# One encoder layer on one core: a gate row multiplied inside the expert loop, the closing norm shared out over three engines, and work moved into three gaps of TensorE

## The reference

```python
u = modulate(rmsnorm(x, norm_mix_g), sh_mix, sc_mix)
q, k, v, xr, yr, fr = split(u @ w_in)
y_na  = neighbourhood_attention(q, k, v, na_rpb)       # 512 channels
y_lru = rglru(conv(xr)) * gelu(yr)                     # 512 channels
y_f   = fourier_mix(fr)                                # 512 channels
g_na, g_lru, g_f = split(sigmoid(u @ w_branch_gate + b))
merged = g_na*(y_na @ w_proj_na) + g_lru*(y_lru @ w_proj_lru) + g_f*(y_f @ w_proj_fnet)
x = x + gt_mix * (merged @ w_out)
u2 = modulate(rmsnorm(x, norm_ffn_g), sh_ffn, sc_ffn)
x = x + gt_ffn * moe_ffn(u2)      # 32 experts, two for each token: w0*y0 + w1*y1
return rmsnorm(x, final_g)
```

## Time and profile before

| | |
|---|---|
| runs shown | 1743.59, 1745.26, 1745.7 us, median 1745.26 |
| profiled execution | 1744.06 us, span from first to last instruction 1742.4 us |
| TensorE busy | 1561.1 us (90%), mean granted clock 0.952 |
| VectorE, ScalarE, POOL busy | 670.7, 480.5 and 518.0 us |
| chain that ended last | PE 82%, DVE 8%, DMA 5%, issue 2% |

### The profile page before, as it was taken

The page is one execution under the profiler, slowest core; times in us unless marked ns, Lnnn a source line. Parts: engine busy times, 40 slices in busy tenths (PEclk is TensorE's granted clock), DMA queues, the critical chain, the costliest instruction groups (busy, mean ns, idle before and its releaser), DMA issues.

```text
span 1742.4 us, 36278 instructions
## 1 busy us (share of the span) xinstructions
PE 1561.1 (90%) x14696; PEld 1125.5 (65%) x14696; DVE 670.7 (38%) x1113; ACT 480.5 (28%) x816; POOL 518.0 (30%) x471
## 2 busy tenths in 40 slices
PE   3899999999979998999999982999999989999950
PEld 3677786777768786878877871555565555555530
DVE  4555534555553244453227743112112111111228
ACT  4465534444631110111013100222222222222214
POOL 3522232423433332233212201233232323323232
PEclk9899999999989999999999975999999999999985
DMA  9560012222123333431206129499999999989745
GB/s 310 157 225 24 25 53 72 70 73 72 38 85 108 114 89 114 150 106 36 89 18 192 49 102 392 163 400 400 400 401 400 399 400 400 400 312 401 280 143 212
DMA packets 177395, 343.10 MB, mean 197 GB/s; under 512 B 30528, under 2 KB 98496, under 8 KB 177296
## 3 DMA queue, kind: packets, MB, share of 16 engines
q1 hardware_dynamic: 144864, 281.90, 44.0%
q0 software_dynamic: 23712, 42.93, 7.4%
q10 hardware_dynamic: 8720, 16.80, 3.1%
HBM read 310.63 MB, written 30.82 MB: 196 GB/s over the span
## 4 chain that ended last, share of the span: by engine, by line
PE 82%; DVE 8%; DMA 5%; issue 2%; ACT 1%; SPq 1%; DVEq 0%; POOL 0%; ACTq 0%; POOLq 0%
PE ps L787 28%; PE ps L1033 19%; PE ps L1044 10%; PE ps L953 7%; PE ps L978 5%; PE ps L851 2%; PE ps L1023 2%; PE ps L824 2%; DMA w_exp<-in_w_exp_up 2%; DMA ada<-in_ada_w 2%; PE ps L877 1%; PE ps L912 1%; PE ps L923 1%; DVE act L1699 1%; PE ps L985 1%
## 5 line engine op out<-in xcount | busy, mean ns | idle before, releaser
L1033 PE MATMUL ps<-w_exp,xT 128*32 128x256 f32 x6272 | 350.0, 381 | 3.8 <-DMA w_exp<-in_w_exp_up 3.5
L787 PE MATMUL ps<-u_hi,w_hi 128*128 128x512 f32 x768 | 310.3, 404 | 5.1 <-DVE u_lo L1392 4.9
L787 PE MATMUL ps<-u_hi,w_lo 128*128 128x512 f32 x768 | 301.9, 393 | 0.0
L787 PE MATMUL ps<-u_lo,w_hi 128*128 128x512 f32 x768 | 301.7, 393 | 0.0
L1033 PEld LDWEIGHTS ps<-w_exp,xT 128*32 128x32 f32 x6272 | 206.2, 110 | 139.0 <-issue 7.0
L1044 PE MATMUL ps<-w_exp,actT 128*32 128x256 f32 x3136 | 179.4, 380 | 0.0
L595 POOL CAST w_hi<-w_raw 128x1024 fp32r<-128x1024 f32 x48 | 60.7, 1265 | 391.1 <-PE ps L787 240.7
L787 PEld LDWEIGHTS ps<-u_hi,w_hi 128*128 128x128 f32 x768 | 146.1, 190 | 44.6 <-issue 10.0
L1699 DVE TENSOR_TENSOR act<-act,ps 64x256 f32<-64x256 f32 x98 | 41.6, 424 | 341.0 <-ACT act L1303 339.5
L697 POOL DMA_INDIRECT xg<-d_u,tok_cur x100 | 100.9, 1009 | 225.7 <-PE ps L1017 209.4
L787 PEld LDWEIGHTS ps<-u_hi,w_lo 128*128 128x128 f32 x768 | 145.8, 190 | 31.4
(11 more groups left out here) (267 smaller groups left out, 2028.1 us busy)
## 6 DMA issues: line engine op xcount, KB each, us to landing
w_exp<-in_w_exp_gate SPq DMA_DIRECT2D x32, 2048.0 KB, 27.2
w_exp<-in_w_exp_up SPq DMA_DIRECT2D x32, 2048.0 KB, 27.0
w_exp<-in_w_exp_down SPq DMA_DIRECT2D x32, 2048.0 KB, 27.1
ada_g<-in_ada_w ACTq DMA_DIRECT2D x32, 512.0 KB, 3.9
d_y<-yb POOLq DMA_DIRECT2D x98, 128.0 KB, 7.4
w_raw<-in_w_in SPq DMA_DIRECT2D x24, 512.0 KB, 4.2
w_raw<-in_w_branch_gate SPq DMA_DIRECT2D x24, 512.0 KB, 4.1
bias<-d_table SPq DMA_DIRECT2D x48, 192.0 KB
```

Source lines behind the costliest of these rows:

```text
L787: ins = pe.matmul(ps[:, 5 + h, :], a[par][:, kc, :], b[:, kc, HF[h]], start=(n == 1), stop=(n == MM))
L1033: last = pe.matmul(ps[CAP * n:CAP * (n + 1), 2 + h, 0:QT], x, w[n // 2][:, off:off + QT], start=(kc == 0), stop=(kc == KC - 1))
```

## The change

It has five parts. In (a) to (c) work goes into places where TensorE stood still, (d) and (e) rebuild the end.

(a) Six of the eight roundings and splits of branch 0 move into the last head pair: pieces 0 and 1 after unit 4, 2 and 3 after unit 5, 4 after unit 6, 5 after unit 7.

(b) `w_out` is rounded and split in four parts for each half instead of two.

(c) TensorE reads 8 of its 32 loop bounds ahead of the list matmuls, 12 behind them and one more ahead of each of the first 12 experts.

(d) `gt_ffn` is laid over the partitions as the loop's output tile has it (`gate_q`, 128x256, plus the bias row `gate_qb`), loaded by eight small transfers of SP. VectorE now empties the down product and multiplies by it in one instruction; ScalarE's copy goes.

(e) At the end all 16 gathers are issued at once into 16 buffers. VectorE adds both weighted rows straight to `x1` (two passes). The last scaling is VectorE's for even tiles; for odd tiles ScalarE multiplies by 1/rms and POOL by `final_g`.

```diff
+        EARLY = {4: (0, 1), 5: (2, 3), 6: (4,), 7: (5,)}
+        EARLY_ALL = 6
+        WO_PIECES = 4
...
+            for q in range(4):
+                own, cols = slice(CAP * q, CAP * (q + 1)), slice(QT * q, QT * (q + 1))
+                sp.dma_start(gate_q[own, :], d_mod[3, cols].partition_broadcast(CAP)).then_inc(ld_gmix, 16)
+                sp.dma_start(gate_qb[own, :], ada_b[0, 5 * D + QT * q:5 * D + QT * (q + 1)].partition_broadcast(CAP)).then_inc(ld_gmix, 16)
...
             for t in range(TT):
-                if t >= YBUF:
-                    pool.wait_ge(fin_ready_x, t - YBUF + 1)
                 for k, y in enumerate((y0, y1)):
...
+            pool.wait_ge(ld_rows, 16 * 6)
+            for t in range(1, TT, 2):
+                pool.wait_ge(fin_scaled, t // 2 + 1)
+                pool.tensor_tensor(res[t][:], res[t][:], fing[:], MUL).then_inc(fin_odd, 1)
...
-                            if t == 0 and kc % 4 == 0:
-                                pe.wait_ge(wo_ready, 2 * h + kc // 4 + 1)
+                            if t == 0 and kc % 2 == 0:
+                                pe.wait_ge(wo_ready, WO_PIECES * h + kc // 2 + 1)
...
+            read_ends(8)
             pe.wait_ge(early_hits, 1)
...
-            pe.wait_ge(starts_ready, 1)
-            ends = [pe.value_load(starts[0:1, i + 1:i + 2], min_val=2 + i, max_val=NPAIR + 1) for i in range(NE)]
+            read_ends(12)
...
+                read_ends(1)
                 r, loads = matrix_at(i, "d")
...
-            def output(h, p):
-                sc.wait_ge(y_ps[h], p + h)
-                sc.wait_ge(st_y[h], p * 16)
-                sc.activation(yb[h][:], ps[:, 6 + h, 0:QT], ACT.Copy).then_inc(y_evac, 1)
...
+            def scale_rows(m):
+                sc.wait_ge(fin_rstd, m + 1)
+                sc.activation(res[m][:], x1[:, m, :], ACT.Copy, scale=rstd2[:, m:m + 1]).then_inc(fin_scaled, 1)
...
+            def split_branch(b, i):
+                kc, h = i // 2, i % 2
+                full = (y_na, lx[:, 2], lx[:, 1])[b][:, kc, HF[h]]
+                if b == 0 and h == 0:
+                    dve.wait_ge(lru_done, kc + 1)
+                dve.wait_ge(br_tmp_ready, 2 * BC * b + i + 1)
+                ch(dve.tensor_tensor(br_lo[:, kc, HF[h]], full, br_tmp[h][:].bitcast(f32), SUB))
+                dve.tensor_copy(br_hi[b][:, kc, HF[h]], br_tmp[h][:]).then_inc(br_ready, 1)
...
+                    if hp == PAIRS - 1:
+                        for i in EARLY.get(r, ()):
+                            split_branch(0, i)
...
+            def output(h, p):
+                dve.wait_ge(y_ps[h], p + h)
+                dve.wait_ge(st_y[h], p * 16)
+                dve.tensor_tensor(yb[h][:], ps[:, 6 + h, 0:QT], gate_q[:], MUL).then_inc(y_evac, 1)
+            dve.wait_ge(ld_gmix, 16 * (2 + 8))
+            ch(dve.tensor_tensor(gate_q[:], gate_q[:], gate_qb[:], ADD))
             with dve.Fori(1, end) as p:
...
-                    ch(dve.scalar_tensor_tensor(y, y1[t % YBUF][:], pair_w[:, 1, t:t + 1], y, MUL, ADD))
-                    ch(dve.tensor_tensor(y, y, gffn[:], MUL))
-                    dve.tensor_tensor(x1[:, t, :], x1[:, t, :], y, ADD).then_inc(fin_ready_x, 1)
+                    ch(dve.scalar_tensor_tensor(x1[:, t, :], y0[t][:], pair_w[:, 0, t:t + 1], x1[:, t, :], MUL, ADD))
+                    dve.scalar_tensor_tensor(x1[:, t, :], y1[t][:], pair_w[:, 1, t:t + 1], x1[:, t, :], MUL, ADD).then_inc(x1_half, 1)
```

More of the change, by code:

```diff
@@ L1001, in _, with read_ends @@
             last.then_inc(rank_ps, 1)
+            pe.wait_ge(starts_ready, 1)
+            ends = []
+            def read_ends(n):
+                for i in range(len(ends), min(len(ends) + n, NE)):
+                    ends.append(pe.value_load(starts[0:1, i + 1:i + 2], min_val=2 + i, max_val=NPAIR + 1))
+            read_ends(8)
             pe.wait_ge(early_hits, 1)
```

130 lines of the change are left out of this document (59 added, 71 removed).

## The result

The changed kernel takes 1738.06 us in the median of six runs (1734.36 to 1742.06), the kernel before 1747.65 in its own six (1743.59 to 1750.53). The ratio is 0.9948, with a 95% interval of 0.9926 to 0.997: 9 us faster, of 17.7 forecast. On another chip the same pair gave 0.9967 (0.995 to 0.9985). Two later runs, 2722.09 us of the changed kernel and 1758.42 us of a variant of it, lie well above all others of their kernels and are left out of every ratio, though not of the medians.

The account below looks back on a forecast made before the run. TensorE's three gaps and VectorE's work at the end were taken as bounds, the expert stage as near its own. 8 + 1.1 + 3.5 + 0 + 5.1 = 17.7 us gave 1727, 8-in-10 range 1719 to 1733.

Parts of the forecast that it names:

- I take nothing: Expert starts: twelve loop-bound readings there were costed at nothing, with 4.1 us lost kept as the bound.
- Gain 11.4 - 3.5 = 8: Attention's end: early splits remove a 9.4 us gap and 2.0 of slow clock, less 3.5 for the delayed softmax.
- Gain 3.5: Expert stage's start: 5.5 us left of 11.66 because the gate row lands late, less 2.0 for the slow clock.
- seam three: TensorE's gap before the first expert, with 11.66 us of reading loop bounds; parts (c) and (d), gain 3.5 us.
- My first rival: Before the first expert: gate row lands by 1080, all 11.66 us are gained, 8.1 more, time 1719; chance 0.12.
- Turns of 12.0 us as before: Expert loop: each turn stays at 12.0 us, also from one expert to the next.
- Seam two: First `wo` matmul, waiting for the first part of `wo_lo`: finer splits, part (b), gain 1.1 us, bounds 0 and 2.
- The end, 5.1: Program's end, part (e): 12.2 us gained, less 7.1 because POOL's multiplications and VectorE's passes exclude each other.
- The copy on VectorE at nothing: Expert loop: VectorE's `output`, about 0.43 us, replaces ScalarE's 0.38 and waits for nothing new; costed at nothing.
- The third rival: Readings cost 0.64 us at each expert and the attention's gap costs the clock: gain 11, time 1734; chance 0.12.
- The fifth: Rival: the parts do nothing because the gaps open again behind; time within 0.2% of before; chance 0.02.
- seam one: Attention's end into the branch loop, where TensorE waited 9.4 us for branch 0's last split; part (a), gain 8 us.

Follow-up runs that it names:

- two splits later: Changed kernel with splits 2 and 3 one unit later and split 5 beside split 4; 1739.93 us, ratio 0.9952 to the kernel before.
- the chain cut short: Changed kernel with three of four adaptive-row loads per block left out, so it computes other numbers; 1742.78 us in all, last projection block at 892.22.

## Why the prediction was wrong

The time was forecast at 1727 and is 1738; the upper end of the range was 1733. Of the 11 us, 2.4 are the kernel before, which is 1747.65 in six runs where the three shown had 1745.26; the other 8 to 9 are missing gain. Step by step:

- **"I take nothing", for twelve readings at the experts' starts.** This step failed. They cost 6.2 us, 0.56 for each that stands between two experts, shown by moving them out of the changed kernel's expert loop and by putting them alone into that of the kernel before. My bound of 4.1 was too low as well, because it let the 3.54 us wait for a matrix take up a share; in none of the eight traces with twelve readings there and the gather in its old place did TensorE wait for one. The row price of 0.64 was near the truth. The Trainium skill, "TensorE: Matmul & The Clock Gate", section "Architectural detail: the array is 16× 32×32, not 1× 128×128", has a queue of 64 instructions, by which the reading would not be noticed; by that rule it is so only where the sequencer is ahead. The runs show both: 0.56 us a reading with the sequencer at the loop's end after 2.9 us, and nothing in nine turns of eleven with 2.2.
- **"Gain 11.4 - 3.5 = 8", for the early splits.** This step failed twice. The local sum was off: the softmax's delay cost 5.1 us, not 3.5 (two splits later), for the clock fell behind the new gap of 5.39 us, which I had only as a bound; the second projection block came 4.7 us earlier in the mean (527.9 and 523.1), not 8. And I followed TensorE only to the next matmul, not to the next thing that it waits for. The wait for `acc` was in the trace of before, 5.8 us at the next branch, with the chain of `ada_g` loads next to the very rows that I used for the port; I took it for a wait of its own and did not ask when TensorE would reach the same chain a block earlier. At the third block 4.2 of the 4.7 us are lost in the mean (21.7 us from the second block instead of 17.5), and at the eleventh 2.3 come back (20.7 instead of 23.0), which leaves 2.8. By the times the splits give nothing that can be measured.
- **"Gain 3.5", seam three.** The mechanism was right, the size was off: 1.1. The gate row was there 27.9 us after the issue of the matrix ahead of it (1057.99 to 1085.9), where I took 26.0 from the earlier trace rows, so that the first hidden transposes came 3.3 us earlier, counted from the first `wo` matmul, and not 5.5; and what followed took 2.3 instead of 2.0: the clock, and a turn of 12.2. My first rival, the gate row as no obstacle, was wrong for this kernel but right as a price: 11.66 in all forecast, 189.8 - 178.4 = 11.4 found on the other queue.
- **"Turns of 12.0 us as before."** This premise was wrong in a way that one trace could not tell: before, too, most turns are 12.2. It bears on the comparison of the two first traces (568.4 and 576.4) and hardly on the times, which hold many executions; that the profiles are 2 us apart and the medians 9 has to do with this and with the first column.
- **Seam two, 1.1** was measured at 1.1 in every trace.
- **The end, 5.1** came out as 3.6. Up to the last output it was 5.2 in the mean (62.1 to 56.9), with the three long passes. But my 3.15 us from the last result to the end of the span is 4.7 here, for POOL's DRAIN. The Trainium skill, "SBUF — State Buffer", section "Who interferes with whom", makes such instructions exclude each other; the trace agrees, 3.24 and 3.47 us beside 1.28. The run without POOL's share shows that POOL makes the passes long, and not the passes themselves. Which of the two gives way is not told by the starts in the profile: in two of the three passes VectorE began 0.05 us ahead of POOL and still was the one that took longer.
- **The copy on VectorE at nothing** was right: the turns of the kernel before don't grow with it (571.5 against 568.4 and 574.2). That this kernel is 4 us faster than before in median, and 6 by the ratio (0.9966), is measured and not explained; its first column and its turns both lie within the scatter.

The third rival (readings at 0.64 and a gap in the attention that costs the clock too, 1734, chance 0.12) was nearest. Both its halves came true in kind (6.2 us where it had 4.1, and 1.6 more in the attention where it had 2.6), and it lacked the row loads and POOL's DRAIN. The fifth, that the gaps open again behind, had 0.02 because it asked for all of it; in part it is what happened in seam one.

The terms as measured don't add up to the 9 us. By the means of the traces they are 2.8 + 1.1 + 1.3 + 3.6 from the four stretches, less 3.0 to 5.9 for the turns (the second or both traces of before), so 3 to 6 us, where the times say 6 and 9. With so few traces, and a first column that scatters by 12 us, the rest can't be placed.

Open: why the first trace of before shows reports at 1.98 us with its gathers issued at 1.41 like all the others. Holding the gather back is enough to have them on time in two kernels; it is not shown to be the only way. By what way the issue of an indirect transfer could hold TensorE's sequencer was not tried, nor was why POOL's DRAIN ends 4.5 us after the multiplication; in the changed kernel with the chain cut short it is 1.8.

## What to carry to other kernels

When a gap is closed, follow the engine to its next wait and ask whether what it waits for moved too: a chain that ran in the shadow of the gap can take the gain, and a run with the chain cut short tells what the gap itself was worth. A small transfer that something waits for does not belong behind large ones on a busy queue; on the idle one it gave 10 us. And read one stage in two traces of the same kernel before pricing anything in it by 0.2 us.

## What the runs showed of the hardware

- In the same code the branch stretch ended between 894.1 and 906.2 us in eight traces, and nearly all of it arose in two of its 23 steps. A VectorE pass with two SBUF inputs takes 0.75 us or, if a subtraction of POOL is under way beside it, 2.8, and the next load waits for it. The five traces in which this befell the second pass over the third load are the five in which the step from the second to the third block was longest (25.4 to 26.1 us against 17.7 to 22.7). That a pass 2 us longer goes with a step some 7 us longer is in part the clock (0.50 behind the wait, in the two traces read); the rest is open.
- A gather issued by POOL 1.4 us after the down matmuls start goes with their report 0.9 us later and TensorE's sequencer 0.7 us later, in all but two turns of 14 traces out of 15; issued at 2.8 us it does neither, in two traces out of two. That is 0.2 us in about half of the turns, and a register reading costs 0.56 us with it and next to nothing without.
- With a multiplication as POOL's last work its DRAIN ended 4.5 us later and put off the end of the program by some 1.7 us, in eight traces of nine (in the ninth it ended 1.8 us later and put off nothing).
